# Scores of a latent-attention branch: two float32 products replaced by five float32r products over high and low parts

## The reference

```python
q = (_rms_norm(q_lat, q_norm_g) @ w_q_up).reshape(bsz, T, 4, 128 + 64)
q_nope, q_pe = q[..., :128], _rope(q[..., 128:], pos)
kv = (_rms_norm(kv_lat, kv_norm_g) @ w_kv_up).reshape(bsz, T, 4, 128 + 128)
k_nope, v = kv[..., :128], kv[..., 128:]
k_pe = _rope(k_rope, pos)                      # one rotary key for all four heads
s = einsum('bqhd,bkhd->bhqk', qn, k_nope) + einsum('bqhr,bkr->bhqk', qr, k_pe)
p = softmax(s * 192 ** -0.5)
o = einsum('bhqk,bkhe->bqhe', p, v)
```

## Time and profile before

| | |
|---|---|
| median of 3 runs | 2166.07 us |
| the profiled execution | 2164.51 us |
| its span | 2162.7 us |
| PE busy | 2141.9 us, 99% |
| DVE busy | 1600.4 us, 74% |
| ACT busy | 1209.3 us, 56% |
| granted clock of TensorE | 1.0 of full speed throughout |

### The profile page before, as it was taken

The page is one execution under the profiler, slowest core; times in us unless marked ns, Lnnn a source line. Parts: engine busy times, 40 slices in busy tenths (PEclk is TensorE's granted clock), DMA queues, the critical chain, the costliest instruction groups (busy, mean ns, idle before and its releaser), DMA issues.

```text
span 2162.7 us, 40159 instructions
## 1 busy us (share of the span) xinstructions
PE 2141.9 (99%) x15748; PEld 1988.8 (92%) x15748; DVE 1600.4 (74%) x2619; ACT 1209.3 (56%) x2060; POOL 427.1 (20%) x450
## 2 busy tenths in 40 slices
PE   9999999999999999999999999999999999999999
PEld 8899989999999999999999889999889888988888
DVE  6777676887578677779857876777876886887874
ACT  5655456665546555566655554555554554665553
POOL 2000212000100011210003530104431550233431
PEclk9999999999999999999999999999999999999999
DMA  7343536355633345454555656545565656435554
GB/s 258 117 133 123 164 117 199 111 176 175 222 117 127 113 141 165 126 181 159 184 193 189 208 186 189 162 153 180 189 191 178 194 186 192 149 120 170 189 188 134
DMA packets 101276, 359.36 MB, mean 166 GB/s; under 512 B 11760, under 2 KB 14960, under 8 KB 100960
## 3 DMA queue, kind: packets, MB, share of 16 engines
q1 hardware_dynamic: 98656, 345.68, 49.5%
q0 software_dynamic: 2000, 10.18, 1.8%
q10 hardware_dynamic: 432, 0.93, 0.1%
HBM read 352.41 MB, written 1.12 MB: 163 GB/s over the span
## 4 chain that ended last, share of the span: by engine, by line
PE 90%; DVE 5%; ACT 2%; DMA 1%; issue 1%; SPq 0%; DVEq 0%; ACTq 0%
PE pd L1428 19%; PE pd L1435 17%; PE pd L1446 16%; PE pd L1443 16%; PE pd L1431 10%; DVE wlo L2337 2%; PE pt L1604 1%; PE ps L1435 1%; PE pd L1620 1%; PE ps L1443 1%; PE ps L1446 1%; PE ps L1579 1%; ACT whi L1892 1%; PE ps L1788 1%; PE pd L1726 1%
## 5 line engine op out<-in xcount | busy, mean ns | idle before, releaser
L2337 DVE TENSOR_TENSOR wlo<-raw,whi 128x1024 fp32r<-128x1024 f32 x618 | 809.6, 1311 | 204.3 <-ACT whi L1892 195.3
L1892 ACT ACTIVATE whi<-raw 128x1024 fp32r<-128x1024 f32 x618 | 651.1, 1055 | 465.0 <-PE pd L1446 271.4
L1435 PE MATMUL pd<-x,whi 128*128 128x272 f32 (+2 forms) x2040 | 608.9, 299 | 1.5 <-DVE tb L2862 1.1
L1446 PE MATMUL pd<-x,wlo 128*128 128x272 f32 (+2 forms) x2031 | 579.5, 285 | 0.5 <-DVE wlo L2337 0.4
L1443 PE MATMUL pd<-x,whi 128*128 128x272 f32 (+2 forms) x2031 | 578.7, 285 | 0.0
L1428 PE MATMUL pd<-x,whi 128*128 128x512 f32 x1288 | 449.9, 393 | 0.0
L1435 PEld LDWEIGHTS pd<-x,whi 128*128 128x128 f32 x2040 | 384.2, 188 | 25.5 <-issue 20.1
L1443 PEld LDWEIGHTS pd<-x,whi 128*128 128x128 f32 x2031 | 383.0, 189 | 1.8
L1446 PEld LDWEIGHTS pd<-x,wlo 128*128 128x128 f32 x2031 | 382.4, 188 | 0.9 <-DVE wlo L2337 0.9
L1431 PE MATMUL pd<-x,wlo 128*128 128x256 f32 x1288 | 361.2, 280 | 0.0
L1428 PEld LDWEIGHTS pd<-x,whi 128*128 128x128 f32 x1288 | 241.8, 188 | 55.0
(11 more groups left out here) (392 smaller groups left out, 3786.8 us busy)
## 6 DMA issues: line engine op xcount, KB each, us to landing
raw<-in_w SPq DMA_DIRECT2D x648, 512.0 KB, 3.7
TA<-scr POOLq DMA_DIRECT2D x2, 1392.0 KB, 11.1
C<-in_c POOLq DMA_DIRECT2D x1, 2368.0 KB, 10.4
TD<-scr POOLq DMA_DIRECT2D x2, 1056.0 KB, 9.2
sw<-tb SPq DMA_DIRECT2D x32, 64.0 KB, 2.9
TD<-scr POOLq DMA_DIRECT2D x2, 768.0 KB, 12.2
h<-in_h SPq DMA_DIRECT2D x4, 272.0 KB, 5.2
out<-result SPq DMA_DIRECT2D x4, 256.0 KB, 2.5
```

Source lines behind the costliest of these rows:

```text
L1435: e.matmul(out, hi, xh, start=begin, stop=False)
L1446: self.block_done(e.matmul(out, lo, xh, start=False, stop=end), c, j)
L1892: e.activation(m.whi[i][:, 0:n], m.raw[c % NRAW][:, 0:n], ACT.Copy).then_inc(*self.up("ac_hi", ("hi", c)))
L2337: e.tensor_tensor(m.wlo[i][:, 0:n], m.raw[c % NRAW][:, 0:n], m.whi[i][:, 0:n].bitcast(F32), ALU.subtract).then_inc(*self.up("dv_lo", ("lo" ...
```

## The change

The plain queries and keys and the rotary queries and keys are each split into a rounded high part and the rest, as the weights already are. A head's product becomes five float32r passes for each 96 queries: plain high by high, high by low key, low query by high key; rotary query by high key, in which the rows that held zeros now hold the low part of the same rotary query; and last the high rotary query by the low key, on the 64 rows of this head alone. ScalarE writes the high parts (`hi_out`, `c_q_hi`, `c_k_hi`), VectorE the low ones (`lo_out`, `c_q_lo`, `c_k_lo`). The sum of `c_rope` goes to the `tn` buffer. The zeros shrink to the 16 padded queries. `load_td` waits for the last scores of branch c too, since the low parts lie in its memory.

```diff
-        for i, t in enumerate(qu[:4] + ku[0::2]):
-            self.step(("dv", "ac", "ac")[i % 3], t.end + 0.1, "copy_out", l, t)
+        for t in qu[:4] + ku[0::2]:
+            self.keep("pd", t.key, t.end + 0.9)
+            self.step("ac", t.end + 0.1, "hi_out", l, t)
+            self.step("dv", t.end + 0.4, "lo_out", l, t)
...
             self.step("dv", e + 1.7, "c_rope", l, i)
+            self.step("ac", e + 2.2, "c_q_hi", l, i)
+            self.step("dv", e + 2.6, "c_q_lo", l, i)
...
         self.step("dv", t + 1.8, "c_krope", l)
+        self.step("ac", t + 2.3, "c_k_hi", l)
+        self.step("dv", t + 2.6, "c_k_lo", l)
...
-            t = self.attend(("c", l, h), max(t, qu[h].end + 1.0, qu[4 + h // 2].end + 2.6, ku[2 * h + 1].end + 0.5)) + 1.5
+            t = self.attend(("c", l, h), max(t, qu[h].end + 1.0, qu[4 + h // 2].end + 3.2, ku[2 * h + 1].end + 0.5)) + 1.5
...
-        self.step("gp", branch[0][7].end + 12.0, "load_td", l)
+        self.step("gp", branch[0][7].end + 13.0, "load_td", l)
...
+        rows = ROWS[h % 2]
         for t in range(3):
-            q = slice(QT * t, QT * t + QT)
-            e.matmul(out[0:QT, t, 0:T1], m.QN[:, h, q], m.KN[:, h, :], start=True, stop=False)
-            last = e.matmul(out[0:QT, t, 0:T1], m.QP[:, h, q], m.KP, start=False, stop=True)
+            q, to = slice(QT * t, QT * t + QT), out[0:QT, t, 0:T1]
+            e.matmul(to, m.QN[:, h, q], m.KN[:, h, :], start=True, stop=False)
+            e.matmul(to, m.QN[:, h, q], m.KL[:, h, :], start=False, stop=False)
+            e.matmul(to, m.QL[:, h, q], m.KN[:, h, :], start=False, stop=False)
+            e.matmul(to, m.QP[:, h, q], m.KP, start=False, stop=False)
+            last = e.matmul(to, m.QP[rows, h, q], m.KPL[rows, :], start=False, stop=True)
...
+    def c_q_hi(self, l, i):
+        e, m, x = self.e, self.m, self.buf("tn", ("pr", l, i))
+        for s in self.ahead(("c_rope", l, i), ("c_zero", l)):
+            e.wait_ge(*s)
+        for r, rows in enumerate(ROWS):
+            o = e.activation(m.QP[rows, 2 * i + r, 0:T1], x[rows, 0:T1], ACT.Copy)
+        o.then_inc(*self.up("ac_split", ("c_q_hi", l, i)))
...
+    def c_q_lo(self, l, i):
+        e, m, x = self.e, self.m, self.buf("tn", ("pr", l, i))
+        for s in self.ahead(("c_q_hi", l, i)):
+            e.wait_ge(*s)
+        for r, rows in enumerate(ROWS):
+            o = e.tensor_tensor(m.QP[ROWS[1 - r], 2 * i + r, 0:T1], x[rows, 0:T1],
+                                m.QP[rows, 2 * i + r, 0:T1].bitcast(F32), ALU.subtract)
...
     def c_zero(self, l):
-        e.memset(m.QP, 0.0).then_inc(*self.up("dv_small", ("c_zero", l)))
+        e.memset(m.QL[:, :, T1:TP].bitcast(F32), 0.0)
+        e.memset(m.QP[:, :, T1:TP].bitcast(F32), 0.0).then_inc(*self.up("dv_small", ("c_zero", l)))
...
-        for r, rows in enumerate(ROWS):
-            o = e.tensor_tensor(m.QP[rows, 2 * i + r, 0:T1], y[rows, :], x[rows, :], ALU.add)
+        e.tensor_tensor(y, y, x, ALU.add).then_inc(*self.up("dv_small", ("c_rope", l, i), ("free", "tn", ("pe", l, i))))
...
     def load_td(self, l):
-        for s in self.ahead(("bias_stored",), *branch_b_done(l)):
+        for s in self.ahead(("bias_stored",), *branch_b_done(l), ("scores", ("c", l, 3))):
```

More of the change, by code:

```diff
@@ L582, in mixer @@
             q = qu[4 + i]
-            e = self.fit(q.end + 0.05, ("tn", ("pe", l, i), 0, 2.6), ("tn", ("pr", l, i), 0.3, 2.6))
+            e = self.fit(q.end + 0.05, ("tn", ("pe", l, i), 0, 2.6), ("tn", ("pr", l, i), 0.3, 3.2))
             self.keep("pd", q.key, e + 0.5)
@@ L1056, in __init__ @@
         self.top = r0
-        self.QN = sb("QN", [128, 4, TP])
-        self.KN, self.KP = sb("KN", [128, 4, T1]), sb("KP", [128, T1])
+        self.QN = sb("QN", [128, 4, TP], F32R)
+        self.KN, self.KP = sb("KN", [128, 4, T1], F32R), sb("KP", [128, T1], F32R)
         self.CV = sb("CV", [128, 3, 512])
@@ L1076, in __init__ @@
         self.top = r2 - 4 * 4 * TP
-        self.QP = sb("QP", [128, 4, TP])
+        self.QP = sb("QP", [128, 4, TP], F32R)
         assert self.top <= r2
+        self.top = r2 - 4 * 4 * (TP + T1) - 2048
+        self.KL = sb("KL", [128, 4, T1], F32R)
+        self.top = r1 + 8704
+        self.QL = sb("QL", [128, 4, TP], F32R)
         self.top = r1
@@ L1093, in __init__ @@
         self.lamv, self.GK = sb("lamv", [128, 16]), sb("GK", [128, T1])
+        self.KPL = sb("KPL", [128, T1], F32R)
         room = [r2 - 21088 + 4096 * i for i in range(5)] + [self.OH_AT + 4096 * i for i in range(3)]
@@ L1224, in projected, with latent_place @@
     room = branch_a_done(l)
+    return m.XA[:, n if name == "c_qa" else 2, :], 1.0, room
+def latent_place(m, t):
+    _, name, n = t.key
     if name == "q_up":
[L1226 to L1229, removed]
+        return m.QN[:, n, 0:T1], m.QL[:, n, 0:T1]
+    return m.KN[:, n // 2, :], m.KL[:, n // 2, :]
 def pair_keys(kind, l, p):
@@ L1587, in c_scores @@
         for s in self.ahead(self.free("ps", key), ("out", (stage, "q_up", h)), ("out", (stage, "kv_up", 2 * h)),
-                            ("c_rope", l, h // 2), ("c_krope", l), ("c_pad", l), ("b_weighed", l, 2)):
+                            ("c_q_lo", l, h // 2), ("c_k_lo", l), ("c_pad", l), ("c_zero", l), ("b_weighed", l, 2)):
             e.wait_ge(*s)
+        rows = ROWS[h % 2]
         for t in range(3):
-            q = slice(QT * t, QT * t + QT)
-            e.matmul(out[0:QT, t, 0:T1], m.QN[:, h, q], m.KN[:, h, :], start=True, stop=False)
-            last = e.matmul(out[0:QT, t, 0:T1], m.QP[:, h, q], m.KP, start=False, stop=True)
+            q, to = slice(QT * t, QT * t + QT), out[0:QT, t, 0:T1]
[4 more added lines that the diff above has]
+            last = e.matmul(to, m.QP[rows, h, q], m.KPL[rows, :], start=False, stop=True)
         last.then_inc(*self.up("pe_scores", ("scores", key)))
@@ L1852, in run @@
             "x_hi": self.x_hi, "z_hi": self.z_hi, "y_sq": self.y_sq, "y_out": self.y_out, "h_sq": self.h_sq,
-            "post_rs": self.post_rs, "copy_out": self.copy_out, "v_out": self.v_out, "v_turned": self.v_turned,
+            "post_rs": self.post_rs, "hi_out": self.hi_out, "c_q_hi": self.c_q_hi, "c_k_hi": self.c_k_hi, "v_out": self.v_out, "v_turned": self.v_turned,
             "silu_tanh": self.silu_tanh, "gate": self.gate, "merged_hi": self.merged_hi, "lam_exp": self.lam_exp,
@@ L1974, in post_rs, with hi_out, c_k_hi @@
                   ("post_rs", stage), ("free", "pt", ("post", stage)))
[L1978 to L1981, removed]
+    def hi_out(self, l, t):
+        e, (dst, _) = self.e, latent_place(self.m, t)
+        for s in self.ahead(("dense", t.key), *branch_a_done(l)):
             e.wait_ge(*s)
-        e.activation(dst, self.buf("pd", t.key)[:, 0:T1], ACT.Copy, scale=scale).then_inc(
-            *self.up("ac_out", ("out", t.key), ("free", "pd", t.key)))
+        e.activation(dst, self.buf("pd", t.key)[:, 0:T1], ACT.Copy).then_inc(*self.up("ac_out", ("hi_out", t.key)))
+    def c_q_hi(self, l, i):
[5 more added lines that the diff above has]
+        o.then_inc(*self.up("ac_split", ("c_q_hi", l, i)))
+    def c_k_hi(self, l):
+        e, m = self.e, self.m
+        for s in self.ahead(("c_krope", l), *branch_a_done(l)):
+            e.wait_ge(*s)
+        e.activation(m.KP, self.buf("tn", ("kd", l))[:, 0:T1], ACT.Copy).then_inc(*self.up("ac_split", ("c_k_hi", l)))
     def v_out(self, l, t, i):
@@ L2305, in run @@
             "lo": self.lo, "gains": self.gains, "x_lo": self.x_lo, "z_hi": self.z_hi, "z_norm": self.z_norm, "z_lo": self.z_lo, "post_mul": self.post_mul,
-            "post_add": self.post_add, "copy_out": self.copy_out, "scaled_out": self.scaled_out, "gate_in": self.gate_in,
+            "post_add": self.post_add, "lo_out": self.lo_out, "c_q_lo": self.c_q_lo, "c_k_lo": self.c_k_lo, "scaled_out": self.scaled_out, "gate_in": self.gate_in,
             "v_out": self.v_out, "v_turned": self.v_turned,
@@ L2394, in post_add, with lo_out, c_k_lo @@
             *self.up("dv_norm", ("h", stage + 1, k)))
[L2398 to L2402, removed]
-            e.wait_ge(*s)
[L2404 to L2408, removed]
+    def lo_out(self, l, t):
+        e, (hi, lo) = self.e, latent_place(self.m, t)
+        for s in self.ahead(("hi_out", t.key), ("b_weighed", l, 2)):
+            e.wait_ge(*s)
+        e.tensor_tensor(lo, self.buf("pd", t.key)[:, 0:T1], hi.bitcast(F32), ALU.subtract).then_inc(
+            *self.up("dv_out", ("out", t.key), ("free", "pd", t.key)))
+    def c_q_lo(self, l, i):
+        e, m, x = self.e, self.m, self.buf("tn", ("pr", l, i))
+        for s in self.ahead(("c_q_hi", l, i)):
+            e.wait_ge(*s)
+        for r, rows in enumerate(ROWS):
+            o = e.tensor_tensor(m.QP[ROWS[1 - r], 2 * i + r, 0:T1], x[rows, 0:T1],
+                                m.QP[rows, 2 * i + r, 0:T1].bitcast(F32), ALU.subtract)
+        o.then_inc(*self.up("dv_split", ("c_q_lo", l, i), ("free", "tn", ("pr", l, i))))
```

(25 more changed lines are left out.)

4 lines of the change are left out of this document (1 added, 3 removed).

## The result

The changed kernel takes 2175.07 us (median of 6 runs, 2171.91 to 2175.61) against 2166.45 us for the kernel before on the same chip (6 runs, 2165.75 to 2167.43): ratio 1.0035, 95% interval 1.0026 to 1.0045. That is 8.6 us more; 5.0 were predicted. Its six executions are of two kinds: four at 2175.0 to 2175.6 us with a mean clock of 0.996, two at 2171.9 and 2172.7 us with 0.998. The profiled execution took 2175.15 us, its span 2173.4 us, its mean clock 0.996.

A forecast was written before the change was run, and what follows sets the result against it. TensorE, busy 99% of the span, was taken to bound the kernel. Its own work, +1.6, and waits for head 0, +3.4, added 5.0 us to 2166.07: 2171.1 us, own range 2169 to 2173, 8 in 10 within 2163 to 2175.

The forecast's parts named there:

- TensorE's own work: Scores of eight heads: shorter float32r passes, but row changes around each 64-row pass, 2.950 us a head against 2.745: +1.6 us.
- (b): Scores: no emptying between float32r passes of 128 and 64 rows, work -6.9, waiting +3.4: 2162.6 us; chance 0.13.
- (d): Row changes in the scores: only the emptying is paid, loads run beside passes: 2166.9 us; chance 0.07.
- Waits for head 0: TensorE waits for `c_q_lo` ahead of head 0's scores, 1.2 and 2.05 us in the two mixers, +3.4 with uncovered loads.
- Rival (a): Head 0's operands come in time, no waiting; only the +1.6 of TensorE's work is left: 2167.7 us; chance 0.18.
- The hidden steps: Added ScalarE (about 3 us a mixer) and VectorE (about 2.7) work, longer bank holds and later `load_td`: no cost.
- rival (c): VectorE falls behind near head 0; head 1 or a dense pass waits too, 2 us more each mixer: 2175 us; chance 0.17.
- The wide range: The range for 8 in 10 on the whole kernel's time: 2163 to 2175 us.

The follow-up runs named there:

- second execution of before: The kernel before the change, unedited, run and profiled a second time: 2166.81 us, span 2165.0.
- head 0 later: Changed kernel with scores due 3.75 instead of 3.2 behind their rotary tile and `c_q_hi` at 2.15, ahead of the gates: 2169.51 us, ratio 1.0014.
- both experiments with the rows: Changed kernel with its fifth pass on all 128 rows, 2164.55 us; kernel before with its rotary product on 64 rows, 2175.59 us.
- The preparation alone: Changed kernel with all high and low parts made, but scores as two float32 products on high parts: 2171.64 us, ratio 1.002; profiled again: 2171.72 and 2169.57 us.
- five full-row passes, first experiment: Changed kernel with the fifth pass of each 96 queries on all 128 rows instead of 64: 2164.55 us, ratio to before 0.999.
- fourth experiment: Kernel before with only its float32 rotary product cut to the 64 rows holding the head's query: 2175.59 us, ratio 1.0042.

## Why the prediction was right and where it was wrong

The sum was +5.0 us; the spans of the second execution of before and of the changed kernel differ by 8.4 us, the medians by 8.6. By its steps:

- *TensorE's own work, +1.6.* Right. A head takes 2.92 us for 2.95 predicted, so +1.4; the change back to the dense blocks costs no more than the others. The pass with 96 columns of weights takes 0.126 us, and the change of rows 0.17 us for 0.173. Rivals (b) and (d) are out: "head 0 later", which has no wait at head 0 and no fall there, still has the work, and both experiments with the rows show the full price, loads included.
- *Waits for head 0, +3.4.* Right in place, cause and size: 1.29 and 2.32 us for 1.28 and 2.13 (1.2 and 2.05 with 0.08 for the uncovered load). ScalarE's two copies of 64 rows took 0.86 us where I had 0.7. Rival (a) is out.
- *What the sum lacked, below:* the wait gave something back. Before, some 19 us behind head 0's scores, TensorE's product of head 0's weights with the values (L1620) waited for a gate that VectorE was writing:
```profile
PE pd L1620 <- DVE GT L2379: 0.3, 1, 0.3
...
PE pd L1620 <- DVE GT L2379: 0.4, 1, 0.4
```
(0.48 and 0.54 us by the starts of the passes.) With head 0 later it is gone in both mixers, -1.0 us. "The preparation alone" is this balance by itself: 1.29 less 0.48 is 0.81, measured 0.79; 2.32 less 0.54 is 1.78, measured 1.73 and 1.67.
- *The step that failed: "TensorE's clock ... nothing here idles it long enough to think of a fall".* I wrote this from a profile in which TensorE never idled for more than 0.7 us behind the load at the start (4.9 us), and then forecast a wait of 2.05 us without returning to it. In 4 of the 6 profiles that have the 2.2 us wait the clock falls right behind it; in none of the 7 without. In the changed kernel's two profiles it stays down for 6.8 us: 5.21 us in the second mixer, less 0.70 of work (4 x 0.175) and 1.78 of net wait, leave 2.7 us. The 3.4 us falls cost less: 1.7 us in the second profile of "the preparation alone", 1.4 with five full-row passes.
- *The fall at 741 us, +1.5 us,* was nowhere in my account. It stands in the execution that I compare, in 4 of the 13 profiles, and in none of the 6 of kernels without the 1.3 us wait in the first mixer (4 of 7 with it). That wait is 550 us earlier and the work between shifts by 0.1 us at most, so I name no link to it; what stands right ahead of each of these falls is the 2.95 us of small passes. Two profiles of the changed kernel differ in it, so it is an execution's own, at least in part.

Together: 1.4 + 3.6 - 1.0 + 2.7 + 1.5 = 8.2 of the 8.4 us. The hidden steps were hidden: TensorE waits for nothing else in the two stretches, neither for low weights nor for a bank. The result lies where rival (c) put it, 2175 us, but not for its reason: VectorE did not fall behind, TensorE got slower. That is luck. The forecast's own range, 2169 to 2173 us, was missed. The wide range reached 8.9 us above the kernel before, and the result is 8.6 above it: it held by 0.3 us, because its edge was this rival's number.

What stays open is what makes the clock fall in one execution and not in the next, and whether the small passes are what brings the falls at 157 and 741 us. The Trainium skill ("TensorE: Matmul & The Clock Gate", What's actually happening) says of a cold start that its length varies between runs of one kernel; the falls here vary between executions too, 4 in 6 behind the 2.2 us wait.

## What to carry to other kernels

Don't cut a pass to the rows that hold data when its neighbours use all 128: with zeros or another useful part in the rest it costs 0.126 us, cut to 64 rows 0.126 + 0.34 (passes of 272 columns). When a step is put between a producer and a matmul, move the matmul by the length of the new chain through all engines, not by a habit, and only for the heads that are short of it. A forecast wait of 2 us on TensorE needs a second term for the clock behind it, with its own probability; check it in windows of a few microseconds, and look there at the size of the passes too, since a busy TensorE can be doing only small ones.

## What the runs showed of the hardware

- A change between passes on 128 and on 64 rows costs 0.17 us: in either direction for float32 (0.62 and 0.63 us from product to product for 0.458, fourth experiment), and 0.34 us for the two together for float32r (first experiment).
- The clock went from 2.4 to 1.2 GHz behind a 2.2 us idle of TensorE in 4 of 6 profiles, for 3.4 us (twice) or 6.8 us (twice), and never behind the 1.3 us idle (0 of 7).
- It also falls where no idle of TensorE is recorded, at or behind 2.95 us of passes on 16 to 64 rows with 16 or 64 columns: at 156 to 158 us in 10 of 13 profiles, at 736 to 741 us in 4 of 13, each time for 3.4 us and 1.5 us of time.
